# A chunked recurrent layer and its expert units: split products in the chunk loop, and the first unit taken by halves

## The chip, the cores and the metric

The kernel runs on one core of a Trainium2 chip. The metric is the device time of one launch in microseconds, the median of three runs. A profiled execution of the same kernel gives the rows shown here. The engines are TensorE (PE in the rows, its weight loads PEld), VectorE (DVE), ScalarE (ACT), GpSimd (POOL) and SyncE (SP), which issues most of the transfers.

## The reference

One layer over 1024 tokens of width 1024, in float32:

```python
z = rmsnorm(x, norm_mix) @ w_in + b_in
mq, mk, mv, mo, mi, mf, aq, ak, av = split(z)
mq, mk = split(silu(causal_conv(concat(mq, mk))))
hm = mlstm_chunkwise(mq, mk, mv, mi, mf)        # 4 heads of 128, a state passed from chunk to chunk
hm = sigmoid(mo) * head_norm(hm) * mlstm_norm
ha = sliding_window_attention(aq, ak, av)       # 8 heads of 64, window 128, sinks, relative bias
x = x + concat(hm, ha) @ w_out
# group top-1 of 4, expert top-2 of 4 inside it: 16 SwiGLU experts, hidden width 512
x = x + moe(rmsnorm(x, norm_ffn))
out = rmsnorm(x, norm_final)
```

## The kernel before, in words

All five engines run programs written by hand, tied by semaphores. A large product is mostly a split product (`split3`, lines 1684 to 1688): each operand is a high part in fp32r and a low part, the rest in fp32r, and three matmuls are summed: high by high, high by low, low by high. High parts are copies by ScalarE, low parts subtractions by VectorE. Where this isn't done, operands are plain float32, and the profile shows two records of a matmul for each.

**Projections and attention** (until about 340 us). 56 jobs on TensorE. The last 33 slots, numbered `j`, carry the attention of 16 blocks of 64 queries and, from slot 25 on, the output gates: ScalarE's tanh of gate `m`, VectorE's product (`s_mog`), SyncE's store to memory. SyncE then loads the upper half of w_out, values, gates back, the lower half of w_out (`s_wout`), and rows of x, in the order of its program.

**Chunk loop** (`for s in range(NT + 3)`, eight chunks of 128 tokens). In step `s` TensorE makes the scores of chunk `s`, transposes the head outputs of chunk `s - 1`, makes the numerators (lines 1916 and 1917), the state update (1922) and the output projection: `project(s - 2, 1)` and `project(s - 1, 0)`, each a half of 512 columns. A half has an attention part (split, `project_attention`) and a recurrent part (line 1846), which is plain:

```python
for k in range(4):
    last = mm(PS[:, 5 + half, :], hT[:, k, P * c:P * c + P], wout[:, k, cols_],
              start=False, stop=(k == 3))
```

ScalarE evacuates the transposed rows into `hT`, makes the decays and scales of the next chunk, and the sum of squares of the new row (line 1036), with `xnb`, of two buffers, as its waste output. VectorE's step: keys `kw`, weighted scores `ptm`, scaled queries `qs`, low attention rows (1255), x2 half (1338), state (1426), router logits (1434), then head norm up to a wait for GpSimd's power (1453), the product with the gate, the exponents of the next chunk (1244), the normed row of an earlier chunk into `xnb`, which SyncE stores, and the top-2 choice of another.

**Way into the expert units.** VectorE builds a table of units (`tab`): each unit is one expert and up to 256 of its tokens, as a first half of 128 and a second, which may be empty (`has_second`). GpSimd gathers the rows of the first unit in two halves (`s_gath[0]`), then those of the next. TensorE transposes them by groups of 256 columns (`x_group`, line 1949), ScalarE and VectorE make high and low parts, and the first products follow. Each unit has six pieces of weights of 1 MB; `lo_piece` releases the load of the next one. The combine weights go to memory (`s_cmbst`), SyncE storing them after the table is ready.

Of the kernel before, what the change touches and what calls it, by code (L numbers as in the profile page):

```python
# [24 lines left out]
P = 128  # L25
# [71 lines left out]
def build(nc, x, norm_mix, w_in, b_in, conv_qk, mlstm_norm, sinks, rel_bias, w_out, norm_ffn,  # L97
# [14 lines left out]
    with ctx:  # L112
# [57 lines left out]
        hT = at("hT", hn_at, [P, H, S])  # L170
        xnb = at("xnb", hn_at + 16 * KB, [P, 2, D])
# [36 lines left out]
        woh_late = at("woh_late", biasb_at, [P, 2, D], f32r)  # L208
# [98 lines left out]
        nfc = stat[:, 52:60]  # L307

# [33 lines left out]
        s_wout = semaphore("s_wout")  # L342
        s_xr0 = semaphore("s_xr0")
# [74 lines left out]
        s_hte = semaphore("s_hte")  # L418

# [106 lines left out]
        def store_xn(sp, c):  # L526
            sp.wait_ge(s_xn, c + 1)
            sp.dma_start(xn_dram[c * P:(c + 1) * P, :], xnb[:, c % 2, :]).then_inc((s_xnst0, s_xnst1)[c % 2], 16)
# [56 lines left out]
        def logits_bank(c):  # L585
            return 4 if c == NT - 1 else 7

# [12 lines left out]
        def _(sp):  # L600
# [96 lines left out]
            store_acc(sp, NT - 1)  # L697
            sp.wait_ge(s_tab, 1)
# [3 lines left out]
            sp.wait_ge(s_cmb, 1)  # L702
            sp.dma_start(comb_dram.rearrange("(t p e) o -> p t (e o)", p=P, e=NE), comb[:, :, :]).then_inc(s_cmbst, 16)
# [31 lines left out]
        def _(pool):  # L735
# [74 lines left out]
            gather_half(1, idx, 0)  # L810
# [8 lines left out]
            pool.dma_start(nfin, bcast(norm_final, D)).then_inc(s_nfin, 16)  # L819
            n_loop = pool.value_load(tab[0:1, 3 * NU:3 * NU + 1], min_val=NE - 2, max_val=MAXU - 1)  # L820

            def unit(u, par, more=1):
# [29 lines left out]
                if more:  # L852
                    pool.wait_ge(s_gath[par], 16 * u + 64)
                    settle(42)
# [36 lines left out]
        def _(act):  # L891
# [49 lines left out]

            for j in range(33):
# [12 lines left out]
                for g in split_after(n):  # L955
                    group_hi(act, g)
                if j % 2 == 0:
# [36 lines left out]
            def weights(s):  # L994
                act.wait_ge(s_arg, s + 1)
                A(arg[:, :, :], arg[:, :, :], ACT.Exp).then_inc(s_e, 1)
                for h in range(H):
                    last = A(ibc[:, h, :], PS[:, 0, P * h:P * h + P], ACT.Exp, bias=rbc[:, h, s:s + 1])
                last.then_inc(s_i, 1)

            def attention_hi(c):
                if c >= 2:
                    act.wait_ge(s_wo, 2 * c - 2)
                A(AQH[:, c % 2, :, :].rearrange("p (k j) w -> p k (j w)", k=2), aqT[:, :, c, :],
                  ACT.Copy).then_inc(s_aqh, 1)
# [12 lines left out]
            for s in range(NT + 3):  # L1018
# [6 lines left out]
                if 1 <= s <= NT:  # L1025
                    act.wait_ge(s_ht, s)
                    A(hT[:, :, P * (s - 1):P * s], PS[:, 3, :].rearrange("p (a b) -> p a b", a=4),
                      ACT.Copy).then_inc(s_hte, 1)
                    if s >= 2:
                        attention_hi(s - 1)  # L1030
                if 2 <= s < NT + 2:
                    c = s - 2
                    act.wait_ge(s_x2, 2 * c + 2)
                    if c >= 2:
                        act.wait_ge((s_xnst0, s_xnst1)[c % 2], 16 * (c // 2))
                    A(xnb[:, c % 2, :], VM[:, c, 0:D], ACT.Square, accum_out=stat[:, c:c + 1]).then_inc(s_ss2, 1)
# [5 lines left out]
                if s + 1 < NT:  # L1042
                    weights(s + 1)
# [68 lines left out]
            A(gm[:, 1, :], gm[:, 0, :], ACT.Exp).then_inc(s_d2, 1)  # L1112
            for g in range(4):
                x_hi(0, g, 0)
            hi_piece(0, 3)
            act.wait_ge(s_tab, 1)
# [31 lines left out]
        def _(dve):  # L1148
# [104 lines left out]
            def attention_lo(c):  # L1253
                dve.wait_ge(s_aqh, c + 1)
                V.tensor_tensor(AQL[:, :, c, :], aqT[:, :, c, :],
                                AQH[:, c % 2, :, :].rearrange("p (k j) w -> p k (j w)", k=2).bitcast(fp32),
                                ALU.subtract).then_inc(s_aql, 1)

            for j in range(33):
# [52 lines left out]
                if j >= 25:  # L1312
                    m = j - 25
                    g, i = m // 4, m % 4
                    dve.wait_ge(s_tanh, 8 + m + 1)
                    V.scalar_tensor_tensor(vo[:, i, :, :],
                                           tb[:, 0:512].rearrange("p (a b) -> p a b", a=2), 1.0,
                                           mlnh[:, 256 * g:256 * g + 256].unsqueeze(1).to_broadcast([P, 2, 256]),
                                           ALU.add, ALU.mult).then_inc(s_mog, 1)
                if j == 30:  # L1320
                    output_lo(0)
                if j == 31:
                    dve.wait_ge(s_cole, 3)
                    exponents(0)
# [3 lines left out]
            dve.wait_ge(s_job, NJ)  # L1328
            V.memset(V1[:, :, :, P:VW], 1.0)
            attention_lo(0)  # L1330
            dve.wait_ge(s_wr, 80)
            V.tensor_tensor(wr[:, :, :], wr[:, :, :], nfc.unsqueeze(2).to_broadcast([P, KD, 20]),
                            ALU.mult).then_inc(s_conv, 1)
# [7 lines left out]
            def normed_rows(c):  # L1341
# [3 lines left out]
                if c >= 2:  # L1345
                    dve.wait_ge((s_xnst0, s_xnst1)[c % 2], 16 * (c // 2))
# [763 lines left out]
```

## Time and profile before

| what | value |
|---|---|
| median of 3 runs | 1027.35 us (1026.7 to 1028.9) |
| the profiled execution's own time | 1029.11 us |
| its span, first to last instruction | 1027.3 us |
| TensorE busy | 952.3 us, 93% |
| VectorE, ScalarE, GpSimd busy | 618.6, 435.5, 268.1 us |
| mean granted TensorE clock | 0.959 of full |
| all records of line 1846 | 128, 57.6 us busy |

Start times count from the first instruction. A matmul's record overlaps the next one's, so the time that it takes is read from start to start. "Idle before <- releaser" is how long an engine stood before a record and what ended the wait. The granted clock is the share of 2.4 GHz that the array was given, so 0.50 is 1.2 GHz.

### The profile page before, as it was taken

Reading aid. Unit: us, or ns where it says so; the run is one execution under the profiler, and the core shown is the slowest. Engines: PE = TensorE matmul, PEld = TensorE weight load, DVE = VectorE, ACT = ScalarE, POOL = GpSimd, SP = SyncE. Lnnn points to the kernel's source line nnn. Section 1 sums busy time; section 2 is a strip of 40 time slices with the busy share of each in tenths; the row PEclk is TensorE's granted clock in tenths of the full one; section 3 lists DMA queues with packets and bytes.
Section 4 is the critical chain, followed back from the end, with each engine's and each line's share of the span. In section 5 each row is a group of like instructions: output and inputs, shape, how many; then the busy total and the mean of one; then the engine's idle time right before and its main releaser. Section 6 shows DMA issues by size and latency. Waiting matters only on the chain.

```text
span 1027.3 us, 15469 instructions
## 1 busy us (share of the span) xinstructions
PE 952.3 (93%) x5005; PEld 770.0 (75%) x5006; DVE 618.6 (60%) x968; ACT 435.5 (42%) x646; POOL 268.1 (26%) x306
## 2 busy tenths in 40 slices
PE   4899999999999799999959999999999999999892
PEld 3498777779999677777647778888888788777671
DVE  5624067775343766666678886565547565575754
ACT  5321244442233222232135774545445654564661
POOL 2300000000000010001025875323316544463523
PEclk8799999999999889999968999999999999999996
DMA  7432111112203912122559999688668887797774
GB/s 276 112 82 68 49 38 29 34 41 73 83 22 123 321 59 78 67 78 97 196 188 318 358 360 380 216 263 251 194 235 251 270 296 204 257 334 250 211 244 181
DMA packets 86290, 184.55 MB, mean 180 GB/s; under 512 B 8371, under 2 KB 29056, under 8 KB 86242
## 3 DMA queue, kind: packets, MB, share of 16 engines
q1 hardware_dynamic: 76114, 153.55, 42.8%
q0 software_dynamic: 9984, 29.84, 11.2%
q8 instruction: 29, 0.48, 0.2%
q10 hardware_dynamic: 144, 0.52, 0.2%
q14 instruction: 19, 0.16, 0.0%
HBM read 151.93 MB, written 31.40 MB: 178 GB/s over the span
## 4 chain that ended last, share of the span: by engine, by line
PE 80%; DVE 9%; issue 4%; ACT 3%; DMA 1%; POOL 1%; DVEq 0%; POOLq 0%; ACTq 0%
PE PS L1686 21%; PE PS L1688 20%; PE PS L1687 20%; PE PS L1846 5%; PE PS L1949 2%; DVE WP L557 1%; PE PS L1931 1%; DVE WL L1488 1%; PE PS L1916 1%; PE PS L1917 1%; PE PS L1818 1%; PE PS L1804 1%; PE PS L1778 1%; PE PS L1694 1%; PE PS L1693 1%
## 5 line engine op out<-in xcount | busy, mean ns | idle before, releaser
L1488 DVE TENSOR_TENSOR WL<-RAW,WH 128x2048 fp32r<-128x2048 f32 x94 | 214.0, 2290 | 93.5 <-ACT WH L1016 91.1
L1016 ACT ACTIVATE WH<-RAW 128x2048 fp32r<-128x2048 f32 x96 | 183.9, 1916 | 27.7 <-PE PS L1688 19.9
L1686 PE MATMUL PS<-WH,XH 128*128 128x512 f32 x400 | 164.4, 411 | 5.6 <-DVE XL L1552 2.4
L1688 PE MATMUL PS<-WH,XL 128*128 128x512 f32 x400 | 157.4, 394 | 0.0
L1687 PE MATMUL PS<-WL,XH 128*128 128x512 f32 x400 | 157.0, 393 | 0.0
L773 POOL TENSOR_TENSOR dst<-dst,stat 128x4 f32<-128x4 f32 x8 | 8.1, 1014 | 351.4 <-DVE dst L1451 351.4
L1686 PEld LDWEIGHTS PS<-WH,XH 128*128 128x128 f32 x400 | 75.7, 189 | 24.0 <-issue 10.5
L781 POOL TENSOR_TENSOR stat<-stat 128x1 f32<-128x1 f32 x92 | 68.0, 747 | 97.8 <-ACT YB L1094 78.7
L1688 PEld LDWEIGHTS PS<-WH,XL 128*128 128x128 f32 x400 | 75.6, 189 | 16.8
L1687 PEld LDWEIGHTS PS<-WL,XH 128*128 128x128 f32 x400 | 76.0, 190 | 13.5
L1686 PE MATMUL PS<-HNH,WP 128*128 128x512 f32 x208 | 84.5, 406 | 0.8 <-issue 0.8
L1688 PE MATMUL PS<-HNH,WP 128*128 128x512 f32 x208 | 82.5, 397 | 0.0
L1687 PE MATMUL PS<-HNL,WP 128*128 128x512 f32 x208 | 82.4, 396 | 0.0
L1686 PE MATMUL PS<-WH,HH 128*128 128x512 f32 x200 | 78.9, 394 | 3.7 <-DVE HL L1564 2.4
L1688 PE MATMUL PS<-WH,HL 128*128 128x512 f32 x200 | 77.9, 390 | 0.0
L1687 PE MATMUL PS<-WL,HH 128*128 128x512 f32 x200 | 77.9, 389 | 0.0
L1686 PE MATMUL PS<-WP,HNH 128*128 128x256 f32 x256 | 73.6, 287 | 0.0
L1687 PE MATMUL PS<-WP,HNH 128*128 128x256 f32 x256 | 72.2, 282 | 0.0
L1688 PE MATMUL PS<-WP,HNL 128*128 128x256 f32 x256 | 72.1, 282 | 0.0
L1047 ACT ACTIVATE XH<-PS 128x512 fp32r<-128x512 f32 (+1 forms) x64 | 32.6, 520 | 65.3 <-PE PS L1949 65.0
L1846 PE MATMUL PS<-wout,hT 128*128 128x512 f32 x128 | 57.6, 593 | 0.0
L805 POOL DMA_INDIRECT gt<-comb_dram,gixc x30 | 50.7, 1691 | 8.5 <-issue 8.2
(324 smaller groups left out, 1781.5 us busy)
## 6 DMA issues: line engine op xcount, KB each, us to landing
RAW<-in_w_gate_dram SPq DMA_DIRECT2D x32, 1024.0 KB, 9.3
RAW<-in_w_up_dram SPq DMA_DIRECT2D x32, 1024.0 KB, 9.9
RAW<-in_w_down_dram SPq DMA_DIRECT2D x32, 1024.0 KB, 5.1
wraw<-in_w_in_dram SPq DMA_DIRECT2D x22, 512.0 KB, 4.6
XT<-in_x_dram SPq DMA_DIRECT2D x8, 512.0 KB, 9.4
vo_dram<-vo SPq DMA_DIRECT2D x16, 256.0 KB, 2.2
wout<-in_w_out_dram SPq DMA_DIRECT2D x4, 1024.0 KB, 8.0
VM<-vo_dram SPq DMA_DIRECT2D x16, 256.0 KB, 5.3
```

The lines of the kernel that those rows point to most:

```text
L557: nc.vector.tensor_tensor(WP[:, g % 2, 4 * h:4 * h + 4, 1, :], wraw[:, h, :, :], WP[:, g % 2, 4 * h:4 * h + 4, 0, :].bitcast(fp32), ALU.su ...
L781: nc.gpsimd.tensor_tensor(stat[:, col:col + 1], stat[:, 32:33], stat[:, 32:33], ALU.add)
L805: nc.gpsimd.indirect_dma_start(gt[:, hf:hf + 1], None, comb_dram, bass.IndirectOffsetOnAxis(ap=rows[:, hf:hf + 1], axis=0)).then_inc(s_gat ...
L1016: A(WH[:, d % SPLITS, :], RAW[:, j, :], ACT.Copy).then_inc(s_whi, 1)
L1047: A(XH[:, par, 2 * g:2 * g + 2, 0:n], PS[:, 6 + g % 2, :].rearrange("p (a b) -> p a b", a=2)[:, :, 0:n], ACT.Copy).then_inc(s_xh, 1)
L1488: V.tensor_tensor(WLS[d % SPLITS][:, :], RAW[:, TURN[d][1] if d else 0, :], WH[:, d % SPLITS, :].bitcast(fp32), ALU.subtract).then_inc(s_w ...
L1686: mm(bank, ah, bh, start=start, stop=False)
L1687: mm(bank, ah, bl, start=False, stop=False)
L1688: return mm(bank, al, bh, start=False, stop=stop)
L1693: mm(bank, HNH[:, k, P * i:P * i + P], w[:, k, :, :], start=(k == 0), stop=False)
L1846: last = mm(PS[:, 5 + half, :], hT[:, k, P * c:P * c + P], wout[:, k, cols_], start=False, stop=(k == 3))
L1949: last = tr(PS[:, 6 + g % 2, UNIT * k + P * hf:UNIT * k + P * hf + P], XGS[par][:, hf, P * (2 * g + k):P * (2 * g + k) + P], ident)
```

## The change

1. Chunk loop: the recurrent part of the output projection becomes a split product for chunks 1 to 7. ScalarE writes `HTH`, VectorE subtracts `HTL` (new wait `s_htl`); once, in steps 1 and 2, ScalarE copies the lower half of w_out into `WMH`, and VectorE subtracts `WML`, over the weights themselves. `xnb` has one buffer in place of two.
2. Order of the way in: the low attention rows of chunk 0 and the exponents move ahead of gate 6 on VectorE; gate 7 and the router weights behind the low part of the output weights; on ScalarE decays and scales of chunk 0 and the copy of output weights move ahead of the last attention output; TensorE waits for that (`s_oe`) later. In the loop the exponents move ahead of the wait for GpSimd's power.
3. First unit: its two gathers have a semaphore each; TensorE, ScalarE and VectorE handle the second half only where it is filled. The combine store moves ahead of the wait for the table on SyncE. TensorE gets 4 and 9 matmuls whose result is not used.

```diff
+        HTH = at("HTH", hn_at, [P, H, P], f32r)
+        HTL = at("HTL", hn_at + 2 * KB, [P, H, P], f32r)
+        xnb = at("xnb", hn_at + 20 * KB, [P, D])
...
@@ SyncE
+            sp.wait_ge(s_cmb, 1)
+            sp.dma_start(comb_dram.rearrange("(t p e) o -> p t (e o)", p=P, e=NE), comb[:, :, :]).then_inc(s_cmbst, 16)
             sp.wait_ge(s_tab, 1)
             n_loop = sp.value_load(tab[0:1, 3 * NU:3 * NU + 1], min_val=NE - 2, max_val=MAXU - 1)
             sp.wait_ge(s_wlo, 1)
             load_piece(0, sp.value_load(tab[0:1, 1:2], min_val=0, max_val=NE - 1))
-            sp.wait_ge(s_cmb, 1)
-            sp.dma_start(comb_dram...).then_inc(s_cmbst, 16)
@@ GpSimd
             gather_half(0, idx, 0)
-            gather_half(1, idx, 0)
+            nc.gpsimd.indirect_dma_start(
+                XGS[0][:, 1, :], None, xn_dram, bass.IndirectOffsetOnAxis(ap=idx[:, 1:2], axis=0)
+            ).then_inc(s_sink, 16)
@@ ScalarE, slots and chunk loop
+                if j == 32:
+                    decays(0)
+                    act.wait_ge(s_o, NQ)
+                    scales(0)
+                    output_hi(1)
...
+                    if j == 31:
+                        act.wait_ge(s_job, NJ)
+                        attention_hi(0)
...
-            attention_hi(0)
-            weights(0)
-            act.wait_ge(*emptied(NJ - 1))
-            act.wait_ge(s_mog, 8)
-            output_hi(1)
...
-                    A(hT[:, :, P * (s - 1):P * s], PS[:, 3, :]...
+                    if s >= 2:
+                        act.wait_ge(s_wo, 2 * s - 2)
+                    A((hT0 if s == 1 else HTH)[:, :, :], PS[:, 3, :]...
...
-                    if c >= 2:
-                        act.wait_ge((s_xnst0, s_xnst1)[c % 2], 16 * (c // 2))
+                    if c >= 1:
+                        act.wait_ge((s_xnst1, s_xnst0)[c % 2], 16 * ((c + 1) // 2))
...
+                if s == 1:
+                    act.wait_ge(s_wout, 32)
+                    act.wait_ge(s_mog, 8)
+                    for i in range(2):
+                        A(WMH[i][:, :, :], wout[:, 2 * i:2 * i + 2, :], ACT.Copy).then_inc(s_wmh, 1)
@@ VectorE
+                if j == 31:
+                    dve.wait_ge(s_job, NJ)
+                    V.memset(V1[:, :, :, P:VW], 1.0)
+                    attention_lo(0)
+                    dve.wait_ge(s_cole, 3)
+                    exponents(0)
+                if 25 <= j < 32:
+                    output_gate(j - 25)
...
+            def split_out_rows(half):
+                w = slice(512 * half, 512 * half + 512)
+                for i in range(2):
+                    dve.wait_ge(s_wmh, i + 1)
+                    V.tensor_tensor(WML[:, 2 * i:2 * i + 2, w], wout[:, 2 * i:2 * i + 2, w],
+                                    WMH[i][:, :, w].bitcast(fp32), ALU.subtract)
...
                 if s == 0:
                     output_lo(1)
+                    output_gate(7)
+                    dve.wait_ge(s_wr, 80)
+                    V.tensor_tensor(wr[:, :, :], ...).then_inc(s_conv, 1)
+                if s == 2:
+                    dve.wait_ge(s_wo, 1)
+                    split_out_rows(0)
                 if 2 <= s <= NT:
                     attention_lo(s - 1)
                 if 2 <= s < NT + 2:
                     x2_half(s - 2, 1)
+                if s == 2:
+                    split_out_rows(1)
+                if 2 <= s <= NT:
+                    dve.wait_ge(s_hte, s)
+                    V.tensor_tensor(HTL[:, :, :], PS[:, 3, :].rearrange("p (a b) -> p a b", a=4),
+                                    HTH[:, :, :].bitcast(fp32), ALU.subtract).then_inc(s_htl, 1)
...
+                    if s + 1 < NT:
+                        exponents(s + 1)
                     dve.wait_ge(s_pow, s + 1)
...
-                if s + 1 < NT:
-                    exponents(s + 1)
@@ TensorE
-            pe.wait_ge(s_oe, NQ)
...
                 for k in range(4):
-                    last = mm(PS[:, 5 + half, :], hT[:, k, P * c:P * c + P], wout[:, k, cols_], ...)
+                    if c == 0:
+                        last = mm(PS[:, 5 + half, :], hT0[:, k, :], wout[:, k, cols_], start=False, stop=(k == 3))
+                    else:
+                        last = split3(PS[:, 5 + half, :], HTH[:, k, :], HTL[:, k, :],
+                                      WMH[k // 2][:, k % 2, cols_], WML[:, k, cols_], False, k == 3)
...
+                if s == 0:
+                    pe.wait_ge(s_oe, NQ)
...
+            def keep_busy(n):
+                for _ in range(n):
+                    mm(PS[:, 5, 0:P], ones[:, :], ident, start=True, stop=True)
+
+            keep_busy(4)
             pe.wait_ge(s_uni, 2)
             mm(PS[:, 2, 8:8 + 3 * NU + 1], ones[0:NE, :], acu[:, :], start=True, stop=True).then_inc(s_cnt, 1)
...
-            pe.wait_ge(s_gath[0], 32)
-            x_group(0, 0)
-            x_group(1, 0)
+            keep_busy(9)
             pe.wait_ge(s_tab, 1)
             n_loop = pe.value_load(tab[0:1, 3 * NU:3 * NU + 1], min_val=NE - 2, max_val=MAXU - 1)
+            first_full = has_second(0)
+            with pe.If(first_full > 0):
+                pe.wait_ge(s_sink, 80)
+                x_half(0, 0, 1)
+                x_half(1, 0, 1)
+            pe.wait_ge(s_gath[0], 16)
+            x_half(0, 0, 0).then_inc(s_xt, 1)
+            x_half(1, 0, 0).then_inc(s_xt, 1)
             pe.wait_ge(s_xl, 2)
             pe.wait_ge(s_wlo, 1)
-            with pe.If(has_second(0) > 0):
+            with pe.If(first_full > 0):
                 gate_up(0, 0, 0, 1)
             gate_up(0, 0, 0, 0).then_inc(s_wused, 1)
-            x_group(2, 0)
-            x_group(3, 0)
+            next_x_group(2, 0, first_full)
+            next_x_group(3, 0, first_full)
```

## Rows read from the trace of the kernel before

**Rows 1.** The page: shares of the chain that ended last

```profile
PE 80%; DVE 9%; issue 4%; ACT 3%; DMA 1%; POOL 1%; DVEq 0%; POOLq 0%; ACTq 0%
```

**Rows 2.** Timeline of TensorE, a middle period: start us, us, record

```profile
416.22 0.39 PE L1916 MATMUL PS<-VM,ptm 128*128 128x129 f32 x2
...
422.20 0.39 PE L1687 MATMUL PS<-WOL,AQH 128*128 128x512 f32 x1
...
424.75 3.59 PE L1846 MATMUL PS<-wout,hT 128*128 128x512 f32 x8
428.18 1.05 PE L1768 MATMUL PS<-qT,kT 128*128 128x128 f32 x8
```

**Rows 3.** Timeline of VectorE in the same period

```profile
414.27 0.68 DVE L1415 SCALAR_TENSOR_TENSOR qs<-ibc,qT 128x512 f32<-128x512 f32 x1
...
422.08 0.24 DVE L1434 SCALAR_TENSOR_TENSOR lg<-PS,stat,rbias 128x20 f32<-128x20 f32 x1 [1.85 <-PE PS L1931]
...
426.02 0.16 DVE L1453 TENSOR_TENSOR dst<-dst 128x4 f32<-128x4 f32 x1 [1.12 <-POOL dst L773]
```

**Rows 4.** Timeline of TensorE: the first attention product of the chunk loop

```profile
342.76 0.77 PE L1686 MATMUL PS<-woh_early,AQH 128*128 128x512 f32 x1 [2.84 <-issue]
```

**Rows 5.** The chain that ended last, from 357 to 368 us

```profile
357.56 1.12 DVE arg L1244 x4
...
359.43 1.09 PE PS L1907 x4
...
361.20 0.77 PE PS L1916 x2
...
367.27 3.63 PE PS L1846 x8
```

**Rows 6.** Windows: stretch, us, busy of PE, PEld, DVE, ACT, POOL, clock, DMA share, GB/s

```profile
342.76:348.00 5.24, 5.24 (x12) 4.10 (x13) 4.31 (x6) 1.70 (x1) 0.00 (x0) 0.50 1.10 366
...
356.66:359.40 2.74, 0.00 (x0) 0.00 (x0) 2.61 (x9) 0.68 (x2) 0.00 (x0) 0.87 1.04 408
```

**Rows 7.** Timeline of VectorE: the low attention rows of chunk 0

```profile
342.01 0.65 DVE L1255 TENSOR_TENSOR AQL<-aqT,AQH 128x512 fp32r<-128x512 f32 x1
```

**Rows 8.** Timeline of ScalarE: the copy of the output weights

```profile
342.54 1.92 ACT L940 ACTIVATE woh_late<-wout 128x2048 fp32r<-128x2048 f32 x1
```

**Rows 9.** Timeline of SyncE's issues: the lower half of w_out

```profile
343.77 2.15 SPq L665 DMA_DIRECT2D wout<-in_w_out_dram  x2
```

**Rows 10.** The chain that ended last, from 531 to 547 us

```profile
531.80 5.34 DMA XG<-xn_dram,idx
537.19 1.98 PE PS L1949 x8
...
540.52 0.99 issue
541.51 0.79 PE PS L1686
...
546.79 0.87 PE PS L1949 x8
```

**Rows 11.** Timeline of VectorE: the last operation of the table

```profile
534.25 0.18 DVE L1525 TENSOR_SCALAR tab<-kk__170 128x28 int32<-128x28 f32 x1
```

**Rows 12.** One tile's rows, XG: the gathers of the next unit

```profile
L784 POOL DMA_INDIRECT XG<-xn_dram,idxc x2: 942/963/984, 537.1 to 538.4; - x2
...
DMA to landing us min/median/max: 7.1/7.2/7.2
```

**Rows 13.** Timeline of TensorE: the first ranks of the router

```profile
507.11 0.43 PE L1865 MATMUL PS<-mk,cst 128*128 128x96 f32 x2 [0.41 <-DVE cum L1372]
```

**Rows 14.** Timeline of ScalarE: the sum of squares of chunk 6

```profile
500.25 1.06 ACT L1036 ACTIVATE xnb<-VM 128x1024 f32<-128x1024 f32 x1 [1.36 <-DVE VM L1338]
```

**Rows 15.** Timeline of SyncE's issues: stores of normed rows 5 and 6

```profile
490.75 13.25 SPq L528 DMA_DIRECT2D xn_dram<-xnb  x2
```

**Rows 16.** One tile's transfers, xn_dram, issued from 480 to 495 us

```profile
DMA to landing us min/median/max: 9.6/9.6/9.6
```

More of the change, by code:

```diff
@@ L206, in build @@
         biasb = at("biasb", biasb_at, [P, 1160])
-        woh_late = at("woh_late", biasb_at, [P, 2, D], f32r)
+        woh_late = at("woh_late", hn_at + 12 * KB, [P, 2, D], f32r)
+        WMH = [at("WMH0", hn_at + 4 * KB, [P, 2, D], f32r), at("WMH1", biasb_at, [P, 2, D], f32r)]
+        WML = at("WML", ring_at, [P, 4, D], f32r)
         AQH = at("AQH", biasb_at + 8 * KB, [P, 2, A_PAIRS, P], f32r)
@@ L418, in build @@
         s_hte = semaphore("s_hte")
+        HTL_BASE = 2 * H - 1
+        s_htl = s_silu
         s_woh = semaphore("s_woh")
@@ L940, in output_hi, with decays, scales, attention_hi @@
                 A(WOH[h][:, :, :], wout[:, 4 + 2 * h:6 + 2 * h, :], ACT.Copy).then_inc(s_woh, 1)
+            def decays(s):
+                act.wait_ge(s_arg, s + 1)
+                A(arg[:, :, :], arg[:, :, :], ACT.Exp).then_inc(s_e, 1)
+            def scales(s):
+                for h in range(H):
+                    last = A(ibc[:, h, :], PS[:, 0, P * h:P * h + P], ACT.Exp, bias=rbc[:, h, s:s + 1])
+                last.then_inc(s_i, 1)
+            def attention_hi(c):
+                if c >= 2:
+                    act.wait_ge(s_wo, 2 * c - 2)
+                A(high_rows(c).rearrange("p (k j) w -> p k (j w)", k=2), aqT[:, :, c, :], ACT.Copy).then_inc(s_aqh, 1)
             for j in range(33):
@@ L1042, in _ @@
                 if s + 1 < NT:
-                    weights(s + 1)
+                    decays(s + 1)
+                    scales(s + 1)
+                if s == 1:
[3 more added lines that the diff above has]
+                        A(WMH[i][:, :, :], wout[:, 2 * i:2 * i + 2, :], ACT.Copy).then_inc(s_wmh, 1)
             def x_hi(u, g, par, n=UNIT):
@@ L1832, in project_attention @@
                 for k in pairs:
-                    split3(PS[:, 5 + half, :], AQH[:, c % 2, k, :],
+                    split3(PS[:, 5 + half, :], high_rows(c)[:, k, :],
                            AQL[:, k // 2, c, P * (k % 2):P * (k % 2) + P],
@@ L1843, in project @@
                     pe.wait_ge(s_hte, c + 1)
+                    if c >= 1:
+                        pe.wait_ge(s_htl, HTL_BASE + c + 1)
                 cols_ = slice(512 * half, 512 * half + 512)
                 for k in range(4):
-                    last = mm(PS[:, 5 + half, :], hT[:, k, P * c:P * c + P], wout[:, k, cols_],
-                              start=False, stop=(k == 3))
+                    if c == 0:
[3 more added lines that the diff above has]
+                                      WMH[k // 2][:, k % 2, cols_], WML[:, k, cols_], False, k == 3)
                 last.then_inc(s_wo, 1)
```

92 lines of the change are left out of this document (39 added, 53 removed).

## The prediction

> **What bounds the kernel now.** I began with the page. The chain that ended last runs through TensorE for 80% of the span and through VectorE for 9% [rows 1], so only time taken from TensorE's own work, or from its waits, can count. The change touches three places, and I read each in the timeline or the chain.
>
> First, the chunk loop (eight chunks of 128 tokens, between 343 and 514 us). In a middle period TensorE goes from one group to the next with no gap. The reader is to see that the eight records of one plain product (four products of 128x512, line 1846) take 428.18 - 424.75 = 3.43 us [rows 2]. The split product ahead of it shows one matmul every (424.75 - 422.20) / 11 = 0.232 us [rows 2].
>
> Second, the way into the loop. TensorE waits 2.84 us before 342.76, and comes back at half clock (0.50 granted, which is 1.2 GHz) [rows 4, 6]. It waits again before the first transposes at 359.43, and again the clock falls [rows 5, 6].
>
> Third, the way out, from the router to the first expert unit: gathers, transposes, evacuations and again 1.2 GHz [rows 10].
>
> **Term 1: split products in the chunk loop.** Four plain products become twelve split matmuls: 12 x 0.232 = 2.78 us in place of 3.43, so 0.65 us less for each half chunk. Chunk 0 stays plain, so 14 halves change. FP8 and Floating Point Precision, section TensorE Precision Notes, of the Trainium skill says that true FP32 takes four passes through the array. Three passes in place of four would save a quarter of 3.43, or 0.86 us, as an estimate from that page, and ten halves would give 8.6 us in place of the 6.5 below. The trace does not bear the ratio out in time: a pass of the plain product takes less than a split matmul does (3.43 / 16 = 0.214 against 0.232) [rows 2]. I go by the rows.
>
> The other engines pay. VectorE gets a subtraction of 128x512 for each chunk (0.6 to 0.7 us, as its neighbours of that size), ScalarE nothing new per chunk. The subtraction stands between the x2 half and the state update, where VectorE later waits 1.85 us for the router logits at 422.08 [rows 3]; it is hidden there. What must stay in time is the chain from the logits to qs, which ended at 414.27 + 0.68 = 414.95, against its use by TensorE at 416.22: 1.27 us of slack [rows 2, 3]. TensorE now comes 1.3 us sooner per period, but VectorE's four exponent instructions (1.12 us, by the row of the same form) move ahead of the wait for GpSimd's pow, where VectorE stands idle 1.12 us [rows 3, 5]. That gives back about 1.0, so 0.9 to 1.0 us of slack stay. If the move gave nothing, the slack would be 0 and the loop would lose at most 0.1 us a period.
>
> Not every half counts. At 507.11 TensorE waits 0.41 us for VectorE's top-2 of chunk 5, which hangs on ScalarE's sum of squares of chunk 6 [rows 13]. That sum now has one buffer in place of two, so it waits for the store of normed rows 5, which lands 9.6 us after its issue at 490.75, behind 4 MB of weights, at about 500.4 [rows 15, 16]. Before, the sum started at 500.25 [rows 14]. TensorE would otherwise have reached it 1.3 us sooner; the store does not move with TensorE. So the two halves of chunk 6 and the first of chunk 7 end in a wait. Chunks 1 to 5 count, 10 x 0.65 = 6.5 us, and the last half of chunk 7, behind that wait, 0.65 us.
>
> The set-up is new: ScalarE copies 128x2048 twice (1.92 us each, as the same copy into woh_late [rows 8]), and VectorE subtracts four pieces of 1024 columns, an estimated 1.2 us each, in step 2. I laid these out from the new times below: the last subtraction and the chunk's low part end about 0.8 us before TensorE has done the attention part of chunk 1 and asks for them. Cost nothing; with that cover gone it costs its overrun, from 0 to 2 us.
>
> **Term 2: the way into the loop.** Before, TensorE waited for the low part of the attention rows, which VectorE wrote at 342.01 behind two gate products and the exponents [rows 7]. Now ScalarE makes the high part at once after the last projection job and VectorE the low part at about 337.6 to 338.2, so the 2.84 us go [rows 4]. The twelve matmuls behind them run at 2.4 GHz (2.8 us in place of the 5.24 us of that window [rows 6]). They end at about 342.75. A new wait follows: the last attention output (s_oe) is now evacuated behind the 1.92 us copy into woh_late, so at about 343.1. TensorE starts its first numerators at 343.15, in place of 348.0, where the window ends, and the first of them no longer at 1.2 GHz: 5.1 us at their end. From here VectorE's chain counts. The exponents (1.12 us, 357.56 [rows 5]) are now done while GpSimd works, so the keys are ready and the transposes start at 353.2 in place of 359.43. The scaled queries follow at 354.3, so the numerators start at 354.35 in place of 361.20: 6.85 us [rows 5].
>
> In between TensorE idles from 351.35 to 353.2, does 0.4 us, and idles 0.7 us more. In the same place it idled 2.7 us before and the clock fell within it (0.87 over the wait) [rows 6]. I take it that it falls again. Then the numerators run at 1.2 GHz as before, and the first plain product starts at about 360.3 in place of 367.27 [rows 5]. Term: 6.95 us. If the clock holds, 9.1 us (numerators 1.8 us in place of 3.6).
>
> The output weights for it are requested later: the store of the last gate now waits for a gate product that stands behind 2.3 us of subtraction, so the two loads are issued at about 346.2 in place of 343.77 [rows 9], and land at 354.5 to 356.6 (8 to 9.3 us). Needed at 358.1 at the earliest: hidden, with 1.5 us to spare.
>
> **Term 3: the first expert unit.** Before, TensorE waited for both gathers, the second landing at 531.80 + 5.34 = 537.14, transposed both halves (1.98 us), waited for evacuations and, 0.99 us, for its branch, and started at 541.51; the first twelve matmuls ran at 1.2 GHz until shortly before 546.79 [rows 10]. That there were twelve and not 24 shows that the unit has one half only. Now only the first gather (one issue of GpSimd earlier) is waited for, and half the columns are transposed and evacuated. The table of units is ready at 534.43 [rows 11] and TensorE reads it before the transposes, so they cannot start before about 535.7. The nine matmuls of no use are 18 records; at 1.2 GHz one takes 1.98 / 8 = 0.25 us [rows 10], so they end at 532.1 + 4.45 = 536.6 and would delay TensorE, at 2.4 GHz at 534.1. I take 536.5 for the start of the transposes and 538.6 for the first expert matmul. The second group of four is done at 547.0 if the first runs cold, 544.2 if warm; but the next unit's gather (issued at 538.39, 7.2 us) lands at 545.6 and does not move [rows 12]. TensorE before reached this point at 546.79 + 0.87 + 2.78 = 550.4 [rows 10]. So the gain is between 1.7 us (cold, late branch) and 4.8 us (the gather); I take 3.6. The four useless matmuls ahead of line 1945 lie in a wait for VectorE that is as long as they are at 1.2 GHz, and cost nothing. The combine store moves up 4.7 us on SyncE, which frees VectorE's wait in front of the third weight piece. In the expert loop itself nothing changes; each load is requested when a piece is used, and moves with it.
>
> **Sum.** 6.5 + 0.65 + 6.95 + 3.6 = 17.7 us. The profiled execution took 1029.11 us for a span of 1027.3; the median of the three runs is 1027.35, so 1027.35 - 17.7 = 1009.7.
>
> **Rivals.**
> (a) The clock holds on the way into the loop. For: the idle time there shrinks. Against: two waits with 0.4 us between them remain. 9.1 in place of 6.95, with the gather bound of 4.8: 21.0 us, 1006.3.
> (b) The useless matmuls run cold and end after the gather, and the set-up in step 2 overruns by 1 us: 6.5 + 0.65 + 5.9 + 1.7 = 14.8 us, 1012.6. For: the records at 537.19 are at 1.2 GHz [rows 10].
> (c) VectorE becomes the bound in the loop. Its chain from the logits to qs would do it, not its work. Half of the split's gain lost: 14 us, 1013.4. Against: the slack above.
> (d) Slower than before: the output weights. TensorE, ScalarE's copies and then every chunk stand behind that load. With 1.5 us of spare and 17.7 us of gain elsewhere it decides only if it lands 19 us later than I think, at 375; at 25 us late the kernel takes 1033. Nothing in the rows shows such a landing.
> (e) The change does not do what it says: the unit's second half is there, and the loop gains alone stay: 14.1 us, 1013.3. The rows speak against it.
>
> **Numbers.** My case 0.50, (a) 0.20, (b) 0.13, (c) 0.07, (e) 0.05, (d) 0.02, and 0.03 for no effect. The range from 1005.3 to 1013.5 takes in (a) with 1.0 us more and (b), (c) and (e). A measurement of this kernel tells about 0.2%, or 2 us, from no change. Faster 0.96, within 0.2% 0.02, slower 0.02.
>
> **What would show it.** The twelve split matmuls of a half take 2.78 us, and a period falls by 1.3 us. No wait in front of the first attention products, and their matmuls at 0.23 us. The numerators of chunk 1 about 7 us sooner. The first expert matmul about 3 us sooner still, against the loop's end. What would make it wrong: a wait of TensorE for the low part of the chunk, for output weights, or for the first x2 half; a clock that falls elsewhere; or the expert loop giving the start back.

## The result, and the profile after

The changed kernel takes **1020.74 us** (median of 7 runs, 1015.58 to 1022.88) against 1027.35: a ratio of 0.9922 (95% interval 0.9903 to 0.9942). It is faster, by 6.6 us in the medians and some 8 by the ratio, where I had forecast 17.7; my range ended at 1013.5. The profiled execution took 1020.74 us, span 1018.9 against 1027.3. A later set of runs gave 1018.3 us and a ratio of 0.9898 (0.9882 to 0.9914). The runs of this kernel lie 7 us apart, those of the kernel before under 4; a possible reason is below.

The chain that ended last, shares by engine: as in [rows 1], with DMA up from 1% to 3%.

```profile
PE 78%; DVE 10%; issue 3%; ACT 3%; DMA 3%; POOL 1%; DVEq 0%; POOLq 0%; ACTq 0%
```

**The way into the loop.** TensorE's timeline; the last two rows answer to the last two of [rows 5].

```profile
341.97 0.49 PE L1972 MATMUL PS<-VM,ptm 128*128 128x129 f32 x2 [0.33 <-ACT aqT L997]
...
352.25 0.63 PE L1961 MATMUL PS<-cst,t 128*128 128x128 f32 x4 [1.76 <-DVE kw L1440]
353.40 0.46 PE L1972 MATMUL PS<-VM,ptm 128*128 128x129 f32 x2 [0.52 <-issue]
...
357.33 3.70 PE L1896 MATMUL PS<-wout,hT 128*128 128x512 f32 x8
```

The first plain product starts 9.9 us sooner (367.27 to 357.33). The numerators and what follows them run from 353.40 to the plain product at 357.33, at full clock. I had them at 1.2 GHz.

**The chunk loop.** One middle period in TensorE's timeline (start us, us, record); it answers to [rows 2].

```profile
375.53 1.05 PE L1816 MATMUL PS<-qT,kT 128*128 128x128 f32 x8
...
382.81 0.60 PE L1911 MATMUL PS<-cst,VM 128*128 128x128 f32 x4
...
387.54 1.96 PE L1987 MATMUL PS<-wr,xnT 128*128 128x20 f32 x16
389.34 0.48 PE L1734 MATMUL PS<-woh_early,AQH 128*128 128x512 f32 x1
...
390.83 0.63 PE L1736 MATMUL PS<-woh_early,AQL 128*128 128x512 f32 x1
391.25 0.63 PE L1734 MATMUL PS<-woh_late,AQH 128*128 128x512 f32 x1
...
393.78 0.40 PE L1734 MATMUL PS<-WMH,HTH 128*128 128x512 f32 x1
...
396.55 0.72 PE L1816 MATMUL PS<-qT,kT 128*128 128x128 f32 x5
```

The split product does what I said: 396.55 - 393.78 = 2.77 us in place of 3.43. But ahead of it the matmuls start 0.43 us apart (390.83 to 391.25) in place of 0.23: TensorE runs at 1.2 GHz from 390.4 to 393.8, with no idle time before. The period is 396.55 - 375.53 = 21.02 us; I expected 19.5. The same stretch in four periods (windows: stretch, us, busy of PE, PEld, DVE, ACT, POOL, clock, DMA share, GB/s):

```profile
387.50:396.50 9.00, 9.00 (x41) 7.53 (x41) 6.99 (x25) 2.09 (x7) 1.76 (x3) 0.81 0.30 104
408.50:417.50 9.00, 9.00 (x42) 7.53 (x41) 6.99 (x25) 2.10 (x7) 1.76 (x3) 0.81 0.31 103
429.50:438.50 9.00, 9.00 (x41) 7.60 (x41) 6.92 (x24) 2.08 (x7) 1.76 (x3) 0.81 0.32 103
450.00:460.00 10.00, 10.00 (x42) 8.38 (x41) 7.44 (x26) 2.60 (x8) 1.76 (x3) 0.66 0.29 105
```

A stretch costs eight matmuls by 0.2 us, 1.6 us; the last is twice as long. In the whole loop this execution gains nothing: 9.9 us ahead at its start, 9.9 us at its end (the slot table's indices on VectorE at 519.31 in place of 529.21).

The kernel before has one such stretch too, in one of its four middle periods. It begins at 464.51, in the same place (three matmuls into the attention part behind the router logits), and TensorE is busy throughout (the clock of 0.78 is a mean: 3.4 of the 7.8 us are at 1.2 GHz):

```profile
464.50:472.30 7.80, 7.80 (x26) 5.10 (x25) 6.26 (x22) 1.66 (x5) 1.01 (x1) 0.78 0.00 0
```

So the change did not bring these stretches in; it made them frequent.

**The end of the loop.** ScalarE's sum of squares answers to [rows 14], TensorE's ranks to [rows 13]:

```profile
489.62 1.06 ACT L1057 ACTIVATE xnb<-VM 128x1024 f32<-128x1024 f32 x1 [3.09 <-DMA xn_dram<-xnb]
```

```profile
496.48 0.71 PE L1917 MATMUL PS<-mk,cst 128*128 128x96 f32 x2 [2.85 <-DVE cum L1406]
```

**The first expert unit.** TensorE's timeline, in place of [rows 10]:

```profile
519.43 2.08 PE L2002 MATMUL PS<-cst,ones 128*128 128x128 f32 x8
521.53 0.71 PE L2006 MATMUL PS<-acu,ones 16*128 16x85 f32 x2
522.17 4.21 PE L2002 MATMUL PS<-cst,ones 128*128 128x128 f32 x18
526.41 0.85 PE L2010 MATMUL PS<-cst,XG 128*128 128x128 f32 x4
528.54 0.50 PE L1734 MATMUL PS<-WH,XH 128*128 128x512 f32 x1 [1.29 <-DVE XL L1599]
...
538.16 0.69 PE L2010 MATMUL PS<-cst,XG 128*128 128x128 f32 x2 [3.38 <-DMA XG<-xn_dram,idxc]
```

The first expert matmul comes 13.0 us sooner (541.51 to 528.54), 3.1 more than the loop's end, and the first twelve run at full clock. Then TensorE waits 3.38 us for the next unit's rows, and the twelve matmuls behind that wait run at 1.2 GHz. They end at 543.86, 9.5 us sooner than before (553.35): the 3.1 us and 0.4 more are given back. The rest of the kernel loses 1.1 us more and the span ends 8.4 us shorter.

GpSimd's second gather of that unit, and VectorE's subtraction beside it:

```profile
528.16 2.28 DVE L1535 TENSOR_TENSOR WL<-RAW,WH 128x2048 fp32r<-128x2048 f32 x1
```

```profile
528.49 2.76 POOL L796 DMA_INDIRECT XG<-xn_dram,idxc  x1 [0.30 <-DMA comb_dram<-comb]
```

### The profile page after: what moved, and what is told of

Same layout as the page of the kernel before. It is cut to its first block, busy times and chain, and to the rows that moved or that the text cites. A ratio compares the mean times of both kernels' runs of the same rounds, so it can differ in the third digit from the quotient of the medians.

```text
span 1018.9 us, 15673 instructions
## 1 busy us (share of the span) xinstructions
PE 950.6 (93%) x5079; PEld 787.0 (77%) x5080; DVE 625.4 (61%) x979; ACT 437.8 (43%) x648; POOL 274.0 (27%) x306
## 4 chain that ended last, share of the span: by engine, by line
PE 78%; DVE 10%; issue 3%; ACT 3%; DMA 3%; POOL 1%; DVEq 0%; POOLq 0%; ACTq 0%
PE PS L1734 22%; PE PS L1736 21%; PE PS L1735 21%; PE PS L2010 2%; DVE WP L566 1%; PE PS L1987 1%; DVE WL L1535 1%; DMA xn_dram<-xnb 1%; DMA XG<-xn_dram,idxc 1%; PE PS L1852 1%; PE PS L1972 1%; PE PS L1826 1%; PE PS L1741 1%; PE PS L1742 1%; PE PS L2040 1%
## 5 line engine op out<-in xcount | busy, mean ns | idle before, releaser
L566 DVE TENSOR_TENSOR WP<-wraw,WP 128x1024 fp32r<-128x1024 f32 x22 | 26.0, 1221 | 41.8 <-ACT WP L561 41.8
```

Of the source, the lines that this page charges most:

```text
L566: nc.vector.tensor_tensor(WP[:, g % 2, 4 * h:4 * h + 4, 1, :], wraw[:, h, :, :], WP[:, g % 2, 4 * h:4 * h + 4, 0, :].bitcast(fp32), ALU.su ...
```

## The experiments

Each kernel was timed beside the kernel before, whose medians were 1027.1 to 1028.0. Kernels of different sets are compared by their ratios.

**One part at a time.** Part 3 alone on the kernel before (rows by halves, useless matmuls, the combine store moved):

```
+ FEWER = (16, 0)
- gather_half(1, idx, 0)
+ indirect_dma_start(XGS[0][:, 1, :], ...).then_inc(s_sink, 16)
+ keep_busy(4) ... keep_busy(9)
```

> The kernel before with the third part alone (first unit by halves, combine store moved up, 13 useless matmuls). Theory: the first expert matmul starts 3 us sooner against the end of the chunk loop, but TensorE then waits 3 to 4 us for the gather of unit 1 and goes on at 1.2 GHz, so nothing is left: 1026 to 1028. Rival, as predicted: 3.6 us stay, 1023.7.

1027.79 us, ratio 1.0003 (0.9991 to 1.0015). The first expert matmul starts at 535.73 in place of 541.51. Of these 5.8 us, 2.6 are there already at the second ranks (521.97 in place of 524.52), ahead of the part that was edited; 3.2 are the unit's. Then:

```profile
545.72 0.44 PE L1960 MATMUL PS<-cst,XG 128*128 128x128 f32 x2 [3.63 <-DMA XG<-xn_dram,idxc]
```

Part 3 alone is worth nothing. All but 0.3 us of its gain is spent in one wait, which the kernel before did not have, and in slow matmuls behind it (550.50 in place of 553.35 at the end of the third twelve).

Parts 2 and 3 without part 1 (the loop's products plain, as in `hT` times `wout` for every chunk):

> The changed kernel with plain products in the chunk loop, all else as changed. Theory: with the split products the clock falls once in nearly every chunk, which eats the 0.65 us per half; so without them the time is that of the changed kernel within 2 us (1018 to 1022), with a period of 20.8 us, one dip at most, and a smaller spread. Rival: the split is worth its 6.5 us and the loss lies elsewhere: 1026 to 1027.

1021.23 us, ratio 0.9932 (0.9918 to 0.9946). That is the changed kernel's gain within the error. Over a whole period the clock holds:

```profile
389.00:410.00 21.00, 21.00 (x117) 15.83 (x116) 14.31 (x48) 5.38 (x12) 1.76 (x3) 1.00 0.20 76
```

(It has one stretch at 1.2 GHz in its four middle periods, from 456.4, as the kernel before has.) So most of the gain of the change is that of the way into the loop. By the ratios the split products add 1.0 us (against 0.9922) to 3.5 us (against 0.9898), with errors of some 2 us, and part 3 nothing.

**What makes the clock fall in the loop.** Between the transposes at 382.81 and the attention part at 389.34 TensorE does only matmuls of 128, 129, 4 and 20 columns. The router logits (16 of 20 columns, 1.8 us) were moved out of that stretch, between attention part and recurrent part, and VectorE's use of them behind the head norm:

```
  def project(c, half, row=-1):
      if c >= 1: project_attention(c, half)
+     if row >= 0: logits(row)
...
-             (logits of c = s - 3 behind state(s))
-             project(s - 1, 0)
+             project(s - 1, 0, s - 3)
```

> The changed kernel with the router logits (16 records of 20 columns) between the attention part and the recurrent part of the first half, not in front of both. Theory: the clock falls because a row of light work (transposes, numerators, logits) comes before the attention part; broken up, the dips go or get fewer: period 19.4 to 20, 1013 to 1016. Rival (the dips come from the dense split products, whatever stands before them): period stays 21.0, 1020 to 1021.

1012.25 us (1011.07 to 1013.16), ratio 0.9843 (0.9828 to 0.9858). The period is 415.89 - 396.45 = 19.44 us, and the clock holds:

```profile
389.00:410.00 21.00, 21.00 (x128) 18.39 (x128) 16.01 (x53) 5.77 (x14) 2.50 (x5) 1.00 0.28 101
410.00:430.00 20.00, 20.00 (x124) 17.58 (x123) 15.03 (x51) 5.39 (x12) 1.76 (x3) 1.00 0.24 87
```

The edit has a price at the end of the loop: TensorE waits 2.07 us for the low attention rows, at 481.63, and runs at 1.2 GHz from 482.6 to 486. The changed kernel has no such wait.

Then the two halves of that edit one by one. TensorE's order alone:

> The kernel after with TensorE's router logits between attention part and recurrent part, and VectorE's use of them left in its old place ahead of the head norm. Theory, that it is the order of TensorE's own work that keeps its clock up: no 1.2 GHz stretch between 369 and 450 us, a period of 19.4 to 19.6 us, 1012 to 1014. Rival, that it was VectorE's part, which no longer stood in a wait for the logits: the period stays at 21 us, 1018 to 1021.

1021.47 us, ratio 0.9943 (0.9929 to 0.9957). Both forecasts fail. The clock is up, as the theory had it (windows), but the period is 418.54 - 397.08 = 21.46 us (TensorE's timeline, and VectorE's of the next period):

```profile
387.50:396.50 9.00, 9.00 (x56) 7.82 (x56) 4.50 (x16) 1.53 (x3) 0.75 (x2) 1.00 0.35 117
```

```profile
406.02 0.63 PE L1971 MATMUL PS<-cst,t 128*128 128x128 f32 x4 [1.08 <-DVE kw L1440]
407.17 0.46 PE L1982 MATMUL PS<-VM,ptm 128*128 128x129 f32 x2 [0.52 <-issue]
```

```profile
415.87 0.24 DVE L1481 SCALAR_TENSOR_TENSOR lg<-PS,stat,rbias 128x20 f32<-128x20 f32 x1 [4.62 <-PE PS L1888]
```

VectorE now waits 4.6 us for the logits, ahead of the head norm and everything behind it, and TensorE waits for the keys that follow. VectorE's move alone:

> The kernel after with VectorE's use of the router logits behind the head norm, and TensorE's logits left where they are, behind the state products. Theory, that the clock goes by the order of TensorE's own work and that VectorE's place costs only where TensorE's logits have moved: the 1.2 GHz stretch of 3 us is there in most periods, the period stays at 21.0 us, and the kernel takes 1018 to 1021 us. Rival, that VectorE's place matters to the clock as well (its earlier head norm and keys let TensorE run without small gaps): fewer stretches at 1.2 GHz, a period of 19.4 us, 1012 to 1014.

1018.46 us, ratio 0.9893 (0.9873 to 0.9913), no different from the changed kernel. The clock falls as before:

```profile
389.00:410.00 21.00, 21.00 (x122) 18.30 (x121) 14.50 (x48) 5.38 (x13) 1.75 (x3) 0.92 0.21 76
```

So TensorE's order sets the clock, VectorE's order the waits, and both are needed. The count over all profiles says the same. With the logits in their old place and split products, 27 of 32 middle periods (eight executions, four each: those with their logits between 387 and 462 us) have a stretch at 1.2 GHz; with plain products, 3 of 12; with the logits moved, none of 20. Why split and plain products differ, with the same small matmuls in front of the attention part, was not settled. The Trainium skill, TensorE: Matmul & The Clock Gate, section HAM oscillation — how this bites in real kernels, ties the falling clock to idle gaps of TensorE. That agrees with the way in, where the clock fell behind waits of 1.76 and 0.52 us in twelve of fourteen executions, and not with the loop: there it fell with no idle time of TensorE in the trace.

**The changed kernel again.**

> The kernel after itself, once more, beside the run above on one chip. It tells how far the 1.2 GHz stretches of its loop repeat. Theory, that they belong to the kernel: again three to five of them between 369 and 514 us, a wait of 3.4 us for unit 1's rows, and 1018 to 1022 us. Rival, that the first profile was unlucky: two or fewer, and 1013 to 1016.

1018.3 us, ratio as above. Again five stretches between 369 and 514 us (391, 413 to 418, 436, 456 and 490). They belong to the kernel. How many there are in one execution varies: where one is missing the period is 19.4 us (395.66 - 376.24 in one run), else 21.0. That may be the reason for the 7 us of spread, since three of the kernels with the moved logits lie within 2 to 3 us; but it isn't shown, for the changed kernel without its useless matmuls (below), which has the stretches, lies within 1 us, and the one with moved logits and plain products within 5. On the way into the loop this execution had the clock low over the numerators (they start at 353.86, the plain product at 359.42), which is the case that I had forecast:

```profile
353.00:358.00 5.00, 4.48 (x26) 4.27 (x24) 0.75 (x2) 1.05 (x2) 0.00 (x0) 0.66 1.07 403
```

**The store of normed rows 5** moved ahead of the four weight loads (`store_xn(sp, NT - 3)` before `load_piece(j, 0)`):

> The changed kernel with the store of normed rows 5 issued ahead of the four weight loads. Theory: ScalarE's sum of squares no longer waits 3.1 us for it, TensorE's wait at the first ranks falls from 2.9 to about 0.5 and the clock stays up there: 3 us less, 1017 to 1018. Rival: the wait moves to the late weights or to VectorE's top-2, gain under 1 us.

1015.32 us (1011.93 to 1018.19), ratio 0.9879 (0.9860 to 0.9898). ScalarE's wait for the store is gone. The profiled execution was that of 1011.93 us, with three stretches at 1.2 GHz up to the ranks in place of four and five (the two profiles of the changed kernel), so it says little on the size; TensorE's first ranks still waited 1.10 us for VectorE. The gain, 0 to 5 us, is not told apart from the scatter.

**Unit 1's rows by halves**, so that its unneeded second half is not waited for:

```
- FEWER = (16, 0)
+ FEWER = (16, 16)
- gather_half(1, idxcs[1], 1)
+ indirect_dma_start(XGS[1][:, 1, :], ...).then_inc(s_sink, 16)
+ with pe.If(next_second > 0): pe.wait_ge(s_sink, 96)
```

> The kernel after, with unit 1's rows gathered by halves with a semaphore each as well, so that TensorE waits for the second half of unit 1 only where unit 1 has one (it has none here). Theory, that term 3 was lost to this wait: TensorE waits 3.38 us in front of the transposes of unit 1, for a half that it does not use, and does the 12 matmuls behind it at 1.2 GHz (about 2.4 us more). The first half was issued one GpSimd instruction earlier, 2.7 us, so the wait falls to under 1.5 us and the clock stays up: j=3 of the first unit 3 to 5 us sooner against the loop's end, 1016 to 1018 us. Rival, that the transfer and not the semaphore is late: both halves share the queues with 4 MB of weights and the first lands only with the second; the wait stays at 3 us and the time at 1020 to 1021.

1014.91 us (1012.29 to 1019.38), ratio 0.9867 (0.9851 to 0.9883). The wait is gone, the clock stays up there, and from the first expert matmul to the fifth group of transposes it takes 546.21 - 532.38 = 13.8 us in place of 547.09 - 528.54 = 18.6:

```profile
532.38 0.67 PE L1736 MATMUL PS<-WH,XH 128*128 128x512 f32 x1 [1.29 <-DVE XL L1601]
...
546.21 0.44 PE L2012 MATMUL PS<-cst,XG 128*128 128x128 f32 x2
```

This is 4.7 us, and the theory's case. But 18.6 is near the long end of what this stretch takes with the unit as changed: the nine profiles of it lie between 15.6 and 18.9 us, the four with the repair between 13.0 and 14.8. The wait itself (2.9 to 3.8 us in six of the nine, 0.2 to 2.1 in three) doesn't fix the price in clock: behind one of 3.16 us the clock stayed up, behind one of 2.92 six matmuls were slow, behind 3.38 and 3.76 all twelve. (This execution, the slowest of the four, had more stretches at 1.2 GHz ahead of the unit.)

**The combine store back in its old place:**

> The kernel after, with the store of the combine weights back behind the first weight piece on SyncE. Theory, that its place matters little to the time: the gather wait of TensorE stays within 1 us of 3.38, and the total at 1019.5 to 1021.5. Rival, that the early store with its 4-byte rows holds the queue that unit 1's rows need: without it there GpSimd's issue of 2.76 us shrinks, the rows land 1.5 to 3 us sooner, and the total is 1017 to 1019; VectorE then waits for the store in front of its third weight piece, and if that wait reaches TensorE the total is above 1022.

1017.86 us (1016.49 to 1022.6), ratio 0.9913 (0.9893 to 0.9933). No difference is to be seen; the issue still took 2.86 us.

**VectorE's subtraction held back** until the gather is issued:

```
  gather_half(1, idxcs[1], 1)
+ gpsimd.tensor_tensor(stat[:, 50:51], ...).then_inc(s_pow, 1)
...
+ dve.wait_ge(s_pow, NT + 1)
  lo_piece(0, 1)
```

> The kernel after, with VectorE's subtraction of unit 0's second weight piece held back until GpSimd has issued the second gather of unit 1. In the kernel after that issue takes 2.76 us and ends 0.8 us after the 2.28 us subtraction that began 0.33 us ahead of it; in the kernel before, with no subtraction beside it, it takes 0.94. Theory, that the subtraction holds the issue up: it takes 0.94 to 1.0 us again, the rows land 1.8 us sooner, TensorE's wait falls from 3.4 to about 1.6 us, the 1.2 GHz stretch behind it stays, and the kernel takes 1.5 to 2.5 us less, 1018 to 1019. Rival, that the queue is slow for other reasons (the combine store or the weights): the issue stays above 2.5 us, 1020 to 1022. Second rival, that the late subtraction delays TensorE's second twelve matmuls by as much: the wait moves, 1020 to 1021.

1015.78 us (1012.88 to 1023.29), ratio 0.9903 (0.9869 to 0.9936), too wide to call. The trace is clear:

```profile
525.74 0.94 POOL L796 DMA_INDIRECT XG<-xn_dram,idxc  x1 [0.30 <-issue]
```

The issue takes 0.94 us, and TensorE's 3.38 us wait falls to a 0.28 us pause at 533.70. About half of that is the issue (2.76 - 0.94 = 1.8 us); the rest is that TensorE comes later, since eight of the unit's first twelve matmuls ran at 1.2 GHz in this execution. In the changed kernel the subtraction ends at 528.16 + 2.28 = 530.44 and the issue at 528.49 + 2.76 = 531.25, 0.81 later. In eleven other runs with the subtraction already under way, by 0.06 to 0.52 us, the issue also ends 0.81 to 0.83 us after it. So GpSimd's issue waits for VectorE's instruction to end. The Trainium skill, SBUF — State Buffer, section SBUF: two separate sides, says that the two engines share a port pair under an exclusive lock, held for a whole instruction, and that a VectorE instruction with two SBUF inputs shuts out a GpSimd instruction that reads SBUF. By that rule, the trace agrees as far as it goes: the subtraction has two such inputs, and the gather takes its row numbers from SBUF (`idxc`). That it's this lock and no other is not shown; nor is what decides where the two begin within 0.02 us of each other, as in the next run.

**Without the useless matmuls:**

> The kernel after without its 13 matmuls of no use. Theory, that they buy the clock and no time: without them the first 12 matmuls of the unit run at 1.2 GHz again (2.4 to 2.7 us more), the transposes start up to 1 us sooner, TensorE reaches unit 1's transposes 1.5 to 2 us later and waits that much less for the gather, and the total stays at 1020 to 1021.5. Rival, that the clock which they lift is worth its price to the end: 1022 to 1024. Second rival, that they delay the unit: 1018.5 to 1019.5.

1014.62 us (1014.23 to 1015.04), ratio 0.9871 (0.9857 to 0.9885). I was wrong: by the ratios the 13 matmuls cost 3 to 5 us. Without them TensorE starts the unit no sooner (the branch on the table sets it), and does the first twelve matmuls at 1.2 GHz. But its transposes run slower as well, VectorE starts its subtraction 0.13 us later than in the run with the combine store in its old place (525.95 there), and the gather, 0.1 us earlier, is not held up:

```profile
526.08 2.33 DVE L1535 TENSOR_TENSOR WL<-RAW,WH 128x2048 fp32r<-128x2048 f32 x1
```

```profile
526.09 0.94 POOL L796 DMA_INDIRECT XG<-xn_dram,idxc  x1 [0.31 <-issue]
```

TensorE comes to unit 1's rows at 534.94 and waits for nothing, in part because its first twelve matmuls were slow. Against the run with the store in its old place, whose trace is within 0.1 us of this one at the second ranks (512.2 against 512.3), the fifth group of transposes is at 541.23 in place of 545.23. That is one profile each; what the useless matmuls buy varies too: with them the first twelve matmuls were at full clock in eight profiles, partly or wholly at 1.2 GHz in five.

**Three repairs at once** (logits, store, halves), with the useless matmuls and without:

> The kernel after with three repairs at once: the router logits between attention part and recurrent part (with VectorE's use of them behind the head norm), the store of normed rows 5 ahead of the four weight loads, and unit 1's rows by halves. Theory, that the three losses are separate: 1012.25 of the first alone, less 2.5 to 5 for the store (with the clock dip behind it gone), less 2 to 4 for the halves: 1004 to 1008 us, a period of 19.44 us and no TensorE wait above 1.5 us between the loop and unit 2. Rival, that behind the loop all goes by the gather of unit 1, which starts when the table of units is there: then the store's gain shifts everything and stays, but the halves give nothing, 1008 to 1010. Second rival, that the store's gain is part of what the first already has: 1011 to 1012.

> The three repairs without the 13 useless matmuls. Where the wait for unit 1's second half is gone, what the useless matmuls do to the clock should show in the time. Theory: without them the unit's first 12 matmuls run at 1.2 GHz (2.4 to 2.7 us more) and start up to 1 us sooner, so 1.5 to 2.5 us slower than with them: 1012.5 to 1013.5. Rival, from the run of the kernel after without them: they shift VectorE's second weight subtraction ahead of GpSimd's second gather and so cost up to 4 us; but that gather is not waited for here, so they should cost nothing here, 1010.5 to 1011.5. Second rival: 1008 to 1009, they cost time in any case.

1010.97 us, ratio 0.9828 (0.9815 to 0.9842), and 1010.99 us, ratio 0.9839 (0.9822 to 0.9855). Both beat both kernels. Beyond the moved logits (0.9843) the other two repairs add 0.4 to 1.5 us by the ratios, which is within the errors. With no wait left to pay for, the useless matmuls neither cost nor gain. The first has a new wait of 1.3 us for VectorE at the transposes of the unit's hidden rows, which takes a part of the gain.

**The same three repairs with plain products in the loop:**

> The three repairs of the run before (logits moved, store earlier, unit 1 by halves) with the plain products of the chunk loop in place of the split ones. Theory, that the split products are worth 0.65 us a half once the clock holds in both kernels: a period of 20.8 us against 19.44, and six to eight us more than the run with split products, 1017 to 1019. Rival, that the logits' new place is worth the 1.4 us a period by itself and the split products nothing: 1010 to 1012.

1019.15 us (1016.48 to 1021.47), ratio 0.9914 (0.9896 to 0.9931), and a period of 411.18 - 390.37 = 20.81 us. Once the clock holds, the split products are worth some 8 us (8.8 and 7.7 by the ratios, against the repaired kernel with and without the useless matmuls).

## Why the prediction was wrong

**Term 1, the split products: the step that failed.** "So 0.65 us less for each half chunk" was right for the product itself (2.77 us) and for the period wherever the clock held (19.4 us, against 19.5 forecast). What failed is the silent assumption that the clock stays at 2.4 GHz once TensorE's work changes. It fell in all four middle periods of this execution, and in most of the others, at a price of 1.6 us, more than the 1.3 us that the period gains. Measured for the loop: 0.0 us in place of 7.15 in the profiled execution, 1.5 in the repeat (7.85 us ahead at its start, 9.30 at its end), 1.0 to 3.5 by the ratios against the kernel with plain products. I had named "a clock that falls elsewhere" as what would make me wrong, without a price or a chance. The kernel before's own stretch at 464.5 would have been a reason to give it both. With the logits moved the term is there, and at least as large as I allowed: some 8 us.

**Rival (c), VectorE's chain,** did not come true in the changed kernel: no wait of TensorE for it between 369 and 489 us. The slack was there, and thin: with 4.6 us of delay in front of the head norm it cost 2 us a period.

**The wait for the store** came as forecast, issue to landing 9.8 us against 9.6, and ScalarE waited 3.09. The store was issued at 479.78, 11.0 us sooner than before, where the loop's start had moved by 9.9. TensorE's wait at the ranks was 2.85 us once and 1.23 the other time, each with a stretch at 1.2 GHz near it that I had not counted.

**Term 2, the way in.** Right in every step: products without a wait, weights on time, transposes behind the keys at 352.25 (353.2), numerators at 353.40 (354.35). Both are within 0.2 us once the 1.1 us are taken off by which this execution was ahead before any edit (337.58 against 338.68 at the last attention matmuls). In it rival (a) came true, and that was luck of the run: 9.9 us, or 8.8 without the 1.1, against the 9.1 of (a). In the repeat, and in all but one of the twelve other kernels with this part of the change, the clock fell as I had taken it; the repeat's gain is 7.85 us, or 7.2 without its own head start of 0.6, against 6.95. The subtractions of the set-up and the output weights stayed hidden, as forecast, so (d) had no basis.

**Term 3, the first unit.** The start gained 3.1 us on the loop's end; the bounds of 1.7 and 4.8 and the 3.6 were of the right size for it, even with the useless matmuls at 1.2 GHz. The step that failed is "the next unit's gather (issued at 538.39, 7.2 us) lands at 545.6 and does not move". It moved: VectorE's subtraction now begins at 528.16, just ahead of the gather's issue at 528.49 (before, 540.43 behind 538.39), the issue takes 2.76 us in place of 0.94, and the gather 9.4 us in all. And I gave the wait for it no price in clock, though [rows 6] show what can follow a wait. Measured: minus 0.4 us in place of 3.6; in the repeat, with a wait of 2.92 and six slow matmuls behind it, plus 1.1. Part of rival (b) came true, the useless matmuls cold, but they did not delay the start. What they cost came, as far as one profile each can show it, from moving VectorE into GpSimd's way.

**The sum:** 9.9 + 0.0 - 0.4 - 1.1 = 8.4 us of span. The last 1.1 us are in the expert loop and its end, where the clock was 0.98 from 860 to 960 us in place of 1.00 (a stretch at 1.2 GHz from 950 to 954); the repeat has no such stretch there, and the cause was not looked for. The median of the kernel before, on which I based the number, is 1.76 us below its profiled execution, which adds the rest of the 11 us.

## What to carry to other kernels

When a change makes one product of a tight loop shorter or splits it, the clock of the neighbouring stretch is a term of the sum: look for long runs of small matmuls next to it, and consider breaking them up with large ones. When a start is moved forward, follow it to the next thing that is waited for, and price that wait with the slow matmuls that may come behind it; here a transfer that nobody needed took the whole gain. Moving a consumer and its producer are two edits: one without the other only trades a slow clock for a wait.

## What the runs showed of the hardware

- TensorE's clock fell to 1.2 GHz with the engine busy throughout, behind 6.5 us of matmuls of 4 to 129 columns, in 27 of 32 middle periods with split products and in 3 of 12 with plain ones. With 1.8 us of them moved elsewhere it stayed at 2.4 GHz, in all of 20.
- An indirect gather issued by GpSimd took 0.94 us alone and 2.6 to 3.0 us beside a 2.28 us subtraction of VectorE that had begun 0.06 us or more ahead; it ended 0.8 us after it, in twelve profiles. Issued 0.01 and 0.02 us behind the subtraction's start, in the two runs without useless matmuls, it was not held up, and the subtraction took 2.33 and 2.34 us.
- All twelve matmuls behind waits of 3.38 and 3.76 us ran at 1.2 GHz; behind waits of 2.92, 3.02 and 3.63 five to seven of them did, and behind one of 3.16 none. One profile does not tell what a wait costs in clock.
